# Moving the causal pooling behind the next block's start, and the decay, alpha and gate products one pair of feature tiles later

## What is computed

```python
h = rms_norm(x, pre_mix_norm)
proj = h @ w_in                       # 1024 -> 2304 columns = 18 feature tiles of 128
u = proj[:, :RWKV_COLS]               # 14 tiles, shifted by one token and mixed with mu
u = u + mu_shift * (token_shift(u) - u)
w_log = -softplus(-(w0 + tanh(wl) @ w_decay_up)) - 0.5
alpha = sigmoid(a0 + al @ w_aaa_up)
g = sigmoid(gl) @ w_gate_up
kk = k * k_k, normed per head; k_mod = k * (1 + (alpha - 1) * k_a)
# last 4 tiles: causal mean over the last 2, 4, 8, 16 tokens, minus the token itself
y_pool[g] = ((cs - lag) / cnt - ug) @ w_pool[g] * pool_scale
```

## Time and profile before

| what | value |
|---|---|
| median of 3 runs | 2773.55 us (2769.07 to 2778.25) |
| the profiled execution | 2772.81 us, span 2771.0 us |
| busy in the span | PE 90%, DVE 56%, ACT 43%, POOL 16% |
| mean granted clock of TensorE | 0.945 of full speed |
| the project phase | from the start to about 635 us |
| its TensorE, from 24 to 635 us | 530.76 us busy of 611 |

### The profile page before, as it was taken

How to read it: one execution, slowest core, us unless ns; L and a number is a source line. 1 busy time by engine, 2 the same in 40 slices (tenths; PEclk the granted TensorE clock), 3 DMA queues, 4 the chain that set the end, 5 groups by cost and what they waited for, 6 DMA issues and landing times.

```text
span 2771.0 us, 41504 instructions
## 1 busy us (share of the span) xinstructions
PE 2487.2 (90%) x16164; PEld 2025.0 (73%) x16164; DVE 1560.8 (56%) x1919; ACT 1197.4 (43%) x1846; POOL 447.9 (16%) x340
## 2 busy tenths in 40 slices
PE   5979798882888868995999999999999999999996
PEld 4757576662777756874888887888878888878885
DVE  1645536464666534443665666666675665666665
ACT  4646465440433334543444444434344444544442
POOL 2625343432222214430000000000000000000000
PEclk9989899995989888997999999999999999999998
DMA  4363634344354416768333354333543334343321
GB/s 141 92 204 92 204 99 160 100 158 123 103 149 128 118 56 205 226 197 260 100 93 104 91 182 122 91 91 97 169 150 101 91 91 150 108 122 91 91 76 76
DMA packets 487924, 353.34 MB, mean 128 GB/s; under 512 B 72380, under 2 KB 438380, under 8 KB 487276
## 3 DMA queue, kind: packets, MB, share of 16 engines
q1 hardware_dynamic: 424748, 284.32, 34.7%
q10 hardware_dynamic: 63040, 67.12, 7.3%
HBM read 271.69 MB, written 79.69 MB: 127 GB/s over the span
## 4 chain that ended last, share of the span: by engine, by line
PE 50%; DVE 3%; ACT 1%; DMA 0%; issue 0%; SPq 0%; ACTq 0%; DVEq 0%
PE p_bank L123 17%; PE p_bank L124 17%; PE p_bank L125 17%; DVE p_acc L2042 1%; DVE p_x L2045 1%; ACT p_dump L1955 1%; DMA p_hT_lo<-scratch_h_lo 0%; DVE p_up_lo L1986 0%; DVE p_dn_lo L1991 0%; DVE p_cv L2011 0%; DVE p_cv L2006 0%; DVE p_cv L2001 0%; DVE p_acc L2031 0%; SPq L1857 0%; ACT p_a_hi L1938 0%
## 5 line engine op out<-in xcount | busy, mean ns | idle before, releaser
L123 PE MATMUL p_bank<-p_hT_hi,p_up_hi 128*128 128x512 f32 x1408 | 549.0, 390 | 25.6 <-DMA p_hT_lo<-scratch_h_lo 25.6
L124 PE MATMUL p_bank<-p_hT_lo,p_up_hi 128*128 128x512 f32 x1408 | 548.7, 390 | 0.0
L125 PE MATMUL p_bank<-p_hT_hi,p_up_lo 128*128 128x512 f32 x1408 | 548.7, 390 | 0.0
L2031 DVE TENSOR_TENSOR p_acc<-p_bank,p_acc 128x512 f32<-128x512 f32 x320 | 221.4, 692 | 198.8 <-PE p_bank L125 191.2
L123 PEld LDWEIGHTS p_bank<-p_hT_hi,p_up_hi 128*128 128x128 f32 x1408 | 264.7, 188 | 82.0 <-issue 25.1
L124 PEld LDWEIGHTS p_bank<-p_hT_lo,p_up_hi 128*128 128x128 f32 x1408 | 264.8, 188 | 55.6
L125 PEld LDWEIGHTS p_bank<-p_hT_hi,p_up_lo 128*128 128x128 f32 x1408 | 264.7, 188 | 55.2
L123 PE MATMUL p_bank<-p_dn_hi,p_a_hi 128*128 128x512 f32 x704 | 281.1, 399 | 15.1 <-DVE p_acc L2028 9.7
L124 PE MATMUL p_bank<-p_dn_lo,p_a_hi 128*128 128x512 f32 x704 | 280.5, 398 | 0.0
L125 PE MATMUL p_bank<-p_dn_hi,p_a_lo 128*128 128x512 f32 x704 | 280.4, 398 | 0.0
L2001 DVE SCALAR_TENSOR_TENSOR p_cv<-p_ub,p_cpar,p_cv 128x512 f32<-128x512 f32 x176 | 127.6, 746 | 251.0 <-ACT p_cv L1927 251.0
(11 more groups left out here) (190 smaller groups left out, 3908.1 us busy)
## 6 DMA issues: line engine op xcount, KB each, us to landing
p_up_raw<-in_w_up SPq DMA_DIRECT2D x176, 512.0 KB, 5.1
p_dn_raw<-in_w_down SPq DMA_DIRECT2D x88, 512.0 KB, 4.1
p_w_raw<-in_w_in SPq DMA_DIRECT2D x72, 512.0 KB, 3.9
p_xin<-in_x SPq DMA_DIRECT2D x8, 1024.0 KB, 6.0
p_m_raw<-scratch_mix SPq DMA_DIRECT2D x16, 512.0 KB, 4.1
p_x<-in_x SPq DMA_DIRECT2D x16, 512.0 KB, 4.7
scratch_x<-p_x ACTq DMA_DIRECT2D x16, 512.0 KB, 2.8
scratch_h_hi<-p_h_hi ACTq DMA_DIRECT2D x16, 512.0 KB, 5.7
```

The lines of the kernel that those rows point to most:

```text
L123: nc.tensor.matmul(out, lhs_hi, rhs_hi, start=start, stop=False)
L124: nc.tensor.matmul(out, lhs_hi, rhs_lo, start=False, stop=False)
L125: return nc.tensor.matmul(out, lhs_lo, rhs_hi, start=False, stop=stop)
L2031: nc.vector.tensor_tensor(dst, bank[:, 4 + n % 4, :], dst, ALU.add).then_inc(s_acc, 1)
```

## The change

The diff moves work and changes no operation. On VectorE, `pool(b, 0)` leaves the end of block `b` and joins the other three groups behind the next block's `low_hT`. On TensorE, the small products of pairs 0 to 3 go to pairs 1 to 4, where the gate products stand ahead of the sums of kk squared. On ScalarE their readers move by two tiles each, the gate's reader by one tile, the exponentials by one tile. On VectorE the scans, the factor of k and the norm's maximum change places with the shifts of tiles 4 to 7.

```diff
 ScalarE, in the loop over f
-                        if f == 1 and b > 0:
+                        if f == 3 and b > 0:
                             pool_out(b - 1)
...
-                        if f == 3:
+                        if f == 5:
                             decays_alphas(b, 0)
-                        if f == 4:
+                        if f == 6:
                             gate_lora(b)
-                        if f == 5:
+                        if f == 7:
                             decays_alphas(b, 1)
-                        if f == 7:
                             kk_squares(b)
-                        if f == 8:
-                            gates(b)
                         if f == 9:
                             kk_root(b)
+                            gates(b)
+                        if f == 10:
                             exp_inverse(b)
-                        if f == 10:
+                        if f == 11:
                             exps(b)
 VectorE
                     low_hT(b)
                     if b > 0:
-                        for x in range(1, PAIRS):
+                        for x in range(PAIRS):
                             pool(b - 1, x)
...
                     for f in range(4):
                         shift(b, f)
+                    shift(b, 4)
                     scan(b, 0)
                     scan(b, 1)
-                    shift(b, 4)
+                    shift(b, 5)
                     scan(b, 2)
                     scan(b, 3)
...
-                    shift(b, 5)
-
+                    shift(b, 6)
                     dve.wait_ge(s_abst, ONE + b * (16 * CH))
...
+                    shift(b, 7)
+
+                    dve.wait_ge(s_sm, ONE + b + 1)
+                    nc.vector.tensor_scalar(norm[:, :], ptr[:, 0, :], 1e-24, None, ALU.max).then_inc(s_nmax, 1)
                     dve.wait_ge(s_ka, ONE + b * PAIRS + PAIRS)
                     dve.wait_ge(s_kkr, ONE + b + 1)
                     nc.vector.tensor_tensor(um[:, K0:K0 + PAIRS, :], um[:, K0:K0 + PAIRS, :], einv[:, :, :], ALU.mult).then_inc(s_km, 1)
-                    shift(b, 6)
-                    shift(b, 7)
-
-                    dve.wait_ge(s_sm, ONE + b + 1)
-                    nc.vector.tensor_scalar(norm[:, :], ptr[:, 0, :], 1e-24, None, ALU.max).then_inc(s_nmax, 1)
...
-                    pool(b, 0)
-                for x in range(1, PAIRS):
+                for x in range(PAIRS):
                     pool(BLOCKS - 1, x)
 TensorE, small(b, pair)
-                    if pair == 0 and b > 0:
+                    if pair == 1 and b > 0:
                         pool_products(b - 1)
-                    if pair == 1:
+                    if pair == 2:
...
-                    if pair == 2:
+                    if pair == 3:
...
-                    if pair == 3:
+                    if pair == 4:
```

## The result

The changed kernel takes 2748.61 us (median of 6 runs, 2747.12 to 2749.6) against 2771.31 us for the kernel before, a ratio of 0.9913 with a 95% interval of 0.9887 to 0.9939. That is 22.7 us less; 34.5 were forecast. The profiled execution has a span of 2747.7 us, 23.3 less than before.

What follows compares the result with a forecast made beforehand. TensorE was taken to bound the kernel, losing some 54 us in waits on VectorE at three block boundaries. Gains of 12 + 22.5 = 34.5 us from 2773.6 gave 2739 us, range 2728 to 2751.

Steps and rivals of the forecast that it cites:

- the 1 us from which the prediction was to count as wrong: Sign of failure: a new TensorE wait over 1 us within a block, before tile 5, v's turning or the pooling's products.
- The first edit: At block boundaries, pool(b, 0) behind low_hT lets the gram start 4.0 us earlier; 12 us over three boundaries.
- The clock's share: Gram at each boundary: 0 to 1.73 us gained if TensorE's granted clock holds; taken as 0.
- The second edit: At boundaries, pooling's products one pair later, behind tiles 2 and 3: 7.5 us earlier each, 22.5 us over three.
- The four product groups have the same length in the new slots: TensorE in the project phase: product groups only change places with tiles; sums of kk squared end at the same place.
- Block 0 "at no cost": Block 0 has no pooling behind it, so its products change places without costing time.
- The covers: Slack in the block: tile 5 not late by 1.7 us, the exponentials' last reader covered by 4.7 us.
- The second rival: Later in the block a reader or weight comes late: 2743 or 2748 us; 10 to 28 us gain, chance 0.16.
- the third: Only the first edit works, the pooling being slower in its new place: 2762 us, chance 0.04.
- the fourth: GpSimd's subtractions hold each of the pooling's 18 instructions, so it lasts 49 us: 2831 us, chance 0.02.

Runs made afterwards that it cites:

- e7: The changed kernel with unused matmuls filling two gaps, four before tile 2 and three before the turn of slice 2: 2741.4 us, ratio to before 0.9888.
- e3: The changed kernel with pool(b-1, 0) placed inside low_hT, between the low halves of slices 2 and 3: 2744.3 us, ratio to before 0.9885.
- e2: The changed kernel with pool(b, 0) put back at the end of VectorE's block, the products still later: 2751.3 us, ratio to before 0.9919.
- e0: The changed kernel, unaltered, timed and profiled again: 2745.3 us, ratio to before 0.9892.
- e1: The kernel before with only pool(b, 0) moved behind the next block's low_hT, products not moved: 2770.8 us, ratio to before 0.9990.
- e5: e3 with the last four slices of tile 1 multiplied behind the last slice of tile 0: 2728.5 us (0.9844), again 2723.9 us (0.9821).
- e4: The changed kernel with the last four slices of tile 1 multiplied behind the last slice of tile 0: 2745.7 us, ratio to before 0.9906.
- e8: e5 with three unused matmuls before the turn of slice 2 at each boundary: 2724.9 us, ratio to before 0.9837.
- e9: e3 with both gaps filled by unused matmuls, before tile 2 and before the turn of slice 2: 2725.3 us, ratio to before 0.9823.

## Why the prediction was right, and where its sum was too large

**The mechanism** was right in its main steps. Two waits on VectorE bounded the boundary; both went; the new ones are those of the forecast: 2.5 us for the low half (2 to 3 were said), 4.1 us for `w_lo` (3 to 4), and 0.95 to 1.01 for the pooling, just at the 1 us from which the prediction was to count as wrong. The measured time is inside the range of 2728 to 2751, near its slow end, but outside the 2734 to 2745 that I gave two thirds of the chances. It lies among the gains of 10 to 28 us, which had 0.16, and the cause that I had given for those, a gain paid back later in the block, did not occur. So the range was wide enough, and the sum behind it was too large. The gain was two thirds of the sum, in the first timing, and four fifths in the second (27.9 us, 2745.25, at the edge of the forecast's own range).

**The first edit**, 4.0 us per boundary: the gram starts 5.08 us behind the first turn and not 9.02, 3.94 us less. The clock's share, 0 to 1.73, of which I took 0, was 0.15 (3.64 against 3.79 us). e7 shows the other bound: with the idle time filled, 2.06.

**The second edit**, 7.5 us per boundary, is the term that was too large. Counted from tile 1's end at 320.11 to 341.08, it took 20.97 us against the 27.6 before: 6.6 gained. The gap before tile 2 is 4.1 and not 3.6, because the pooling holds up GpSimd's `w_lo`; I had allowed for the hold on VectorE only, though the kernel before shows the other direction too: its next `w_lo`, at 337.76, took 2.79 us under an addition of the pooling. In e3, where the first group is done by then, it is 3.7. The wait for the pooling is 0.95 and not 0.5: the four groups took 19.5 us, where 17 to 19 were forecast. Tiles 2 and 3 themselves were right at 12.8 us (12.65 in the sum), but that number was a reading of block 0 of one profile, and it was luck that it came out again: they take 11.00 at full clock (the sum compares with 11.4, a row that includes the slow start behind a small product), and e2 had 11.00 at two boundaries behind nearly the same gap.

**"The four product groups have the same length in the new slots"** failed by 0.5 us a block behind each boundary. At pair 4 the gate products now stand right ahead of the sums of kk squared, and the sums start 3.5 us behind them (378.42 to 381.94), where a tile starts 3.0 behind such a group.

```profile
378.42 3.60 PE L717 MATMUL p_pm<-p_um,p_wgate 128*128 128x512 f32 x8
381.94 1.07 PE L783 MATMUL p_ptr<-p_tmp,p_head_sums 128*32 128x512 f32 x8
```

Block 0 loses nothing by it: from the end of tile 3 to the next block it takes 94.18 us against 94.14, since tiles 4 and 5 no longer stand behind a product. So a boundary gave 3.94 + 0.2 + 6.6 - 0.5 = 10.3 us (the 0.2 lie between the gram and the end of tile 1), and the table has 10.3 for blocks 2 and 3 and 9.6 for block 1, where tiles 2 and 3 took 13.3 us and not 12.8. The forecast said 11 to 13 each.

**Block 0 "at no cost"**: it was 1.6 us longer, and in e0 as well (128.66 before, 130.26). Of that, 0.7 us are gone by the start of tile 2 and 0.9 more by the end of tile 3. I took the clock behind the gap of 3.67 us from one profile. It is not fixed. The gap of e1, of the same 3.67 us at the same place, left the clock at the upper level, and e0's brought it down for over 5 us:

```profile
46.50:57.60 11.10, 11.08 (x50) 8.94 (x50) 3.61 (x3) 3.68 (x5) 8.11 (x5) 1.00 0.33 96
```

```profile
46.70:52.00 5.30, 5.29 (x13) 4.19 (x14) 3.36 (x2) 0.00 (x0) 4.68 (x3) 0.50 0.46 132
```

Tiles 2 and 3 took 11.1 us in e1 and 12.65 in the kernel before. The order of work up to the end of tile 3 in block 0 is the same in e1, e0 and the kernel before, and behind tile 3 the lengths are equal, so I put the 1.6 us down to the clock and the drift of single executions, and not to the change. Why it fell in one and not in the other is open.

**The covers** held. The last exponential ends at 399.55 us and its reader starts at 404.66, 5.1 us of cover against the 4.7 estimated.

```profile
397.65 1.90 ACT L470 ACTIVATE p_cum<-p_cum 128x2048 f32<-128x2048 f32 x1
...
404.66 4.36 DVE L692 TENSOR_TENSOR p_alpha<-p_alpha,p_einv 128x2048 f32<-128x2048 f32 x1
```

Tile 5 didn't wait either. The second rival, a gain paid back later in the block, did not happen by its mechanism, though the time came out at one of the numbers it gave (2748). Nor did the third and the fourth: the pooling lasts 337.83 - 318.31 = 19.5 us, and only six of its 18 instructions are held.

**The remaining 5 us** between 28.6 and 23.3 are spread over unchanged code. 2.4 of them are in the phase's tail (from the last block's gram to the recurrence's first matmul 48.4 us and not 46.0), where the turns and the products ran more at the low clock. In e0 the same tail took 45.5 us, and from the gram on the two profiles of e5 differ by over 20, so single executions differ by more than this.

## What to carry to other kernels

Where a fast engine waits twice on a slow one in a row, moving work past the first wait only lengthens the second (e1: 4.0 us gained, 3.8 given back); the consumer has to move with it. Before an edit is judged by itself, ask which wait ends just behind the one that it removes: e3 and e4 gave 0 and 1 us each, and 12.6 us together. A change in one phase is best measured by that phase in the profile, between marks on the engine that bounds it, when other phases vary from one execution to the next by as much as the gain.

## What was unexpected of the hardware

A gap can cost TensorE more than its length. Behind most gaps of 2.1 to 4.1 us it was granted 1.2 GHz for some us, but not behind all. Gaps of 3.65 to 3.68 us did so in e0 and at e2's block 2, and did not in e1 or at e2's blocks 1 and 3. In e8 a gap of 2.12 us at block 2 was followed by 0.50 (window from 308.5), and one of 2.11 at block 3 by 1.00 (window from 442.7):

```profile
308.50:311.90 3.40, 3.40 (x10) 2.62 (x9) 3.12 (x5) 1.76 (x3) 1.44 (x1) 0.50 0.94 281
442.70:447.00 4.30, 3.69 (x15) 2.71 (x15) 3.98 (x6) 2.31 (x5) 1.45 (x1) 1.00 0.38 144
```

What decides it was not found. Filling the gaps with matmuls of no use kept the gram and tiles 2 and 3 at 2.4 GHz, and made the kernel faster where nothing else was in the way: e9 does more work than e3 and its project phase is 19 us shorter.

The hold between VectorE and GpSimd works in both directions: the same subtraction took 2.35 us when it came first and 2.81 to 2.91 when it came under an instruction of the pooling. The Trainium skill states the rule in SBUF — State Buffer, "Who interferes with whom": which side is blocked goes by the order of issue, not by the kind of the operation. The trace agrees, with a VectorE instruction held in one place and a GpSimd one in the other.
